# The second pair of experts is loaded without waiting for the first tile's gathered rows

## Chip, cores and metric

The kernel runs on one core of one Trainium2 chip. The metric is the device time of one execution in microseconds (us), as a median over several executions. Engines are called PE (TensorE), PEld (its weight loads), ACT (ScalarE), DVE (VectorE), POOL (GpSimd) and SP (SyncE, which here only issues DMAs). DMAs issued by SP appear as queue q1, those issued by POOL as q0.

## The reference, cut to what matters

Two transformer blocks run one after the other on 512 tokens of width 1024, in float32. The first is a state-space mixer beside forgetting attention and a gated MLP. The second is retention beside sliding-window attention, then a mixture of experts, then a gated per-layer embedding. The change concerns the mixture of experts:

```python
def hierarchical_moe(h, w_rg, b_rg, w_re, b_re, w_gate, w_up, w_down):
    ...
    g_sel = jnp.argmax(g_prob, axis=-1)                  # one of 4 groups
    ...
    top_p, top_i = lax.top_k(jax.nn.softmax(e_in_group, axis=-1), TOP_K)   # 2 of its 8 experts
    ...
    for grp in range(N_GROUPS):
        sl = slice(grp * EXPERTS_PER_GROUP, (grp + 1) * EXPERTS_PER_GROUP)
        hid = jax.nn.silu(jnp.einsum('td,edf->tef', hf, w_gate[sl])) * jnp.einsum('td,edf->tef', hf, w_up[sl])
        y = y + jnp.einsum('tef,efd->td', hid * combine[:, sl, None].astype(hid.dtype), w_down[sl])
    return y.reshape(b, s, d)
```

There are 32 experts, each with a gate and an up matrix of 1024 x 256 and a down matrix of 256 x 1024, and every token uses two of them.

## The kernel before, in words

**Up to the experts.** All dense weights stream through a ring of 8 buffers (`raw`), in units of 256 KB that SP loads. ACT and DVE split each unit into a high part (`hi`) and a low part (`lo`), and PE multiplies with both, so that a product takes three matmuls (lines 341 to 343). PE counts finished units in the semaphore `unit_used`. The stream's last units before the experts are the router's and those of the per-layer embedding (`ple0`, `ple1`). With the last matmul on `ple1` the count reaches `MOE_AT`, and from then on nobody reads `raw`, `hi` or `lo` for the whole expert stage.

**Routing.** DVE turns the router's logits into a table `sidx` of token rows for each tile of work (lines 1081 to 1183), with two small stretches of PE in between (the ranks of the tokens at line 920, the table itself at line 930). Before that POOL has stored the normalised rows `xn3` in device memory as `xg_d`.

**Expert tiles.** An expert gets up to 64 rows; two experts make a tile of 128 rows. There are `MAIN` = 16 main tiles (expert j with expert j + 16) and `OVER` = 8 overflow tiles for experts that got more than 64 rows, run in the order main, main, overflow. For tile n:
- POOL gathers its rows from `xg_d` into `XE[n % 2]` with an indirect DMA (`gather`, line 1269; semaphores `xe_full[0]` and `xe_full[1]`). Gathers 0 and 1 are issued as soon as `sidx` stands; gather n + 2 follows when PE has transposed tile n. Rows out of bounds are skipped.
- PE transposes them (`turn`, lines 934 to 941), DVE scales them into `XT` (line 1188), PE multiplies with the gate and up weights (`gate_up`, line 958: 32 matmuls), ACT and DVE form the hidden values, PE multiplies with the down weights (`down`, line 977: 16 matmuls), and POOL scatters the result to `ye_d` (line 1277).

PE's loop for tile n is gate_up(n), turn(n + 1), down(n - 1), then two transposes (line 991).

**Expert weights.** The pair j of experts has 6 MB of weights. SP loads them into one of two slots: four pieces of 1024 KB for gate and up (line 1348), then 2048 KB for down (line 1354). Slot 0 has memory of its own. Slot 1 lies over the ring, 48 KB a partition at exactly the place of `raw`, `hi` and `lo`. So pair 0 may be loaded while the dense stream still runs, and pair 1 only once `unit_used` stands at `MOE_AT`. In the kernel before, SP waits for one more thing ahead of pair 1: for `xe_full[0]`, the landing of gather 0. A later pair's piece is loaded when PE has used the same piece of the pair two before it. For overflow tiles, POOL loads weights into a third slot with indirect DMAs (line 1284) that skip everything where no expert overflows.

**Who waits for what ahead of the first gate_up.** PE waits for `xe_full[0]` in `turn(0)`, then for the count 48 of `b2c` (ACT's copies of the embedding at line 1026 raise it to 48; its later work at lines 1035 and 1039 raises it to 58), then for `XT` of tile 0, then for piece 0 of the weights:

```python
            turn(0)
            pe.wait_ge(b2c, 48)
```

The program of SP and what calls it, with the numbers of the profile's lines:

Of the kernel before, what the change touches and what calls it, by code (L numbers as in the profile page):

```python
# [69 lines left out]
def nth_split(u):  # L70

    return u if u < MOE_AT + XU else u - XU
# [30 lines left out]
def bass_two_blocks(nc, x, cst_d, rows_d, mats_d, bias_d, ident_d, identb_d, maskT_d, maskL_d, rb_d, tri_d,  # L103
                    pT_d, wstream, wexp, out):
    ctx = ExitStack()
    with ctx:
        def sem(name):
            return ctx.enter_context(nc.semaphore(name))
# [195 lines left out]
        xe_full = [sem(f"xe_full{i}") for i in range(2)]  # L304
# [1007 lines left out]
        @block.sync  # L1312
        def _(sp):
            for t in range(T):
                sp.dma_start(X[:, t, :], x[t * P:(t + 1) * P, :]).then_inc(x_loaded[t], 16)
            for c in range(RING):
                sp.dma_start(raw[:, c, :], wstream[c]).then_inc(raw_full[c], 16)

            def reload(u0, n=RING):

                for u in range(u0, u0 + n):
                    if u - RING >= MOE_AT:
                        sp.wait_ge(unit_used, u + 1 - RING)
                    else:
                        sp.wait_ge(lo_ready, u + 1 - RING)
                    sp.dma_start(raw[:, u % RING, :], wstream[u if u < MOE_AT else u - XU]).then_inc(raw_full[u % RING], 16)

            rounds = MOE_AT // RING
            with sp.Fori(1, rounds) as i:
                for c in range(RING):  # L1330
                    sp.wait_ge(lo_ready, i * RING + (c + 1 - RING))
                    sp.dma_start(raw[:, c, :], wstream[bass.ds(i * RING + c, 1)].rearrange("a p n -> (a p) n")
                                 ).then_inc(raw_full[c], 16)
            reload(rounds * RING, MOE_AT - rounds * RING)
            both = wexp.rearrange("(e m) p n -> m p e n", e=2)

            def gate_up(j):

                if j == 0:
                    sp.wait_ge(m_s, 8)  # L1340
                    sp.wait_ge(lo_ready, MOE_AT - PIECES)
                elif j == 1:
                    sp.wait_ge(unit_used, MOE_AT)
                    sp.wait_ge(xe_full[0], 16)
                for i in range(PIECES):
                    if j >= 2:
                        sp.wait_ge(unit_used, MOE_AT + (j - 2) * PIECES + i + 1)
                    sp.dma_start(slots[j % 2][:, :, 2 * i:2 * i + 2, :].rearrange("p e c n -> p e (c n)"),
                                 both[j][:, :, 1024 * i:1024 * i + 1024]).then_inc(raw_full[(j * PIECES + i) % RING], 16)

            def down(j):
                if j >= 2:
                    sp.wait_ge(dn_mm, 2 * ORDER.index(j - 2) + 2)
                sp.dma_start(slots[j % 2][:, :, 8:12, :].rearrange("p e c n -> p e (c n)"),
                             both[j][:, :, 4096:6144]).then_inc(dn_full[j % 2], 16)

            for j in range(0, MAIN, 2):
                gate_up(j)
                if j == 0:
                    down(j)  # L1360
                gate_up(j + 1)
                if j:
                    down(j)
                down(j + 1)
            sp.wait_ge(unit_used, MOE_AT + XU)
            reload(FIRST["pg0"], RING)
            for i in range(2):
                sp.wait_ge(ye_st[i], 16 * (TILES // 2))
            for t in range(T):
                sp.dma_start(YG[:, :, :].rearrange("p (k t) d -> p k t d", k=2)[:, :, t, :],  # L1370
                             ye_d.rearrange("(k t p) d -> p k t d", k=2, t=T)[:, :, t, :]).then_inc(x_loaded[t], 16)
            for u in range(FIRST["pg1"], NU):
                sp.wait_ge(lo_ready, nth_split(u - RING) + 1)
                sp.dma_start(raw[:, u % RING, :], wstream[u - XU]).then_inc(raw_full[u % RING], 16)
            for t in range(T):
                sp.wait_ge(out_ready, 4 + t + 1)
                sp.dma_start(out[t * P:(t + 1) * P, :], X[:, t, :]).then_inc(out_stored, 16)
            sp.wait_ge(out_stored, 16 * T)
# [1122 lines left out]
```

## Time and profile before

| what | value |
|---|---|
| median of 3 runs | 1678.85 us (1678.52 to 1680.55) |
| the profiled execution's own time | 1680.54 us |
| its span, from the first to the last instruction | 1678.6 us |
| mean granted clock of PE | 0.97 |
| PE busy | 1560.0 us, 93% of the span |
| DVE, ACT, POOL busy | 809.5, 617.5, 137.9 us |

The profiled execution lies 1.7 us above the median of the three runs and 1.9 us above its own span. A busy share is an average over stages with different limits, so the stage of the change is read by itself. The granted clock is the share of full speed that the chip allowed PE in a stretch; 0.50 is 1.2 GHz and 1.00 is 2.4 GHz. "To landing" is the time from the issue of a DMA to the increment of its semaphore.

### The profile page before, as it was taken

Reading aid. Unit: us, or ns where it says so; the run is one execution under the profiler, and the core shown is the slowest. Engines: PE = TensorE matmul, PEld = TensorE weight load, DVE = VectorE, ACT = ScalarE, POOL = GpSimd, SP = SyncE. Lnnn points to the kernel's source line nnn. Section 1 sums busy time; section 2 is a strip of 40 time slices with the busy share of each in tenths; the row PEclk is TensorE's granted clock in tenths of the full one; section 3 lists DMA queues with packets and bytes.
Section 4 is the critical chain, followed back from the end, with each engine's and each line's share of the span. In section 5 each row is a group of like instructions: output and inputs, shape, how many; then the busy total and the mean of one; then the engine's idle time right before and its main releaser. Section 6 shows DMA issues by size and latency. Waiting matters only on the chain.

```text
span 1678.6 us, 20983 instructions
## 1 busy us (share of the span) xinstructions
PE 1560.0 (93%) x7452; PEld 1133.3 (68%) x7452; DVE 809.5 (48%) x1472; ACT 617.5 (37%) x1182; POOL 137.9 (8%) x156
## 2 busy tenths in 40 slices
PE   5989999989999999999999998999997999999947
PEld 4777778745787888888887887777785333333336
DVE  4766764577334666664324354654456122222263
ACT  4556543367324455553223313454335200000122
POOL 0004200010000000000000001000001122221100
PEclk9999999999999999999999999999998999999969
DMA  5232233221232333333323322221243999999331
GB/s 183 69 128 90 73 120 95 60 73 39 72 98 76 96 99 94 100 94 97 99 82 102 100 70 63 70 69 59 86 170 137 407 411 400 388 386 369 129 150 50
DMA packets 93168, 232.93 MB, mean 139 GB/s; under 512 B 15952, under 2 KB 16208, under 8 KB 88864
## 3 DMA queue, kind: packets, MB, share of 16 engines
q1 hardware_dynamic: 79296, 209.75, 36.3%
q0 software_dynamic: 13072, 21.77, 3.9%
q8 instruction: 53, 0.87, 0.2%
q10 hardware_dynamic: 720, 0.33, 0.1%
q14 instruction: 27, 0.22, 0.0%
HBM read 282.05 MB, written 16.84 MB: 178 GB/s over the span
## 4 chain that ended last, share of the span: by engine, by line
PE 84%; DVE 9%; ACT 3%; issue 1%; DMA 1%; POOL 1%; SPq 0%; ACTq 0%; DVEq 0%; POOLq 0%
PE ps L341 20%; PE ps L343 19%; PE ps L342 19%; PE ps L958 10%; PE ps L977 5%; PE ps L940 1%; DVE lo L336 1%; PE ps L444 1%; DVE acc L1929 1%; PE ps L1594 1%; PE ps L1582 1%; PE ps L1568 1%; PE ps L544 1%; PE ps L1446 1%; DVE HTl L409 1%
## 5 line engine op out<-in xcount | busy, mean ns | idle before, releaser
L336 DVE TENSOR_TENSOR lo<-raw,hi 128x512 fp32r<-128x512 f32 x304 | 208.6, 710 | 313.8 <-ACT hi L330 313.2
L330 ACT ACTIVATE hi<-raw 128x512 fp32r<-128x512 f32 x304 | 184.8, 632 | 383.8 <-PE ps L343 382.4
L341 PE MATMUL ps<-HTh,lo 128*128 128x512 f32 x688 | 274.3, 399 | 20.0 <-DVE HTl L409 6.4
L342 PE MATMUL ps<-HTl,hi 128*128 128x512 f32 x688 | 271.6, 395 | 0.0
L343 PE MATMUL ps<-HTh,hi 128*128 128x512 f32 x688 | 271.5, 395 | 0.0
L341 PEld LDWEIGHTS ps<-HTh,lo 128*128 128x128 f32 x688 | 131.4, 191 | 50.9 <-DVE HTl L409 12.4
L343 PEld LDWEIGHTS ps<-HTh,hi 128*128 128x128 f32 x688 | 131.6, 191 | 28.1
L342 PEld LDWEIGHTS ps<-HTl,hi 128*128 128x128 f32 x688 | 131.6, 191 | 27.1
L341 PE MATMUL ps<-hi,HTl 128*128 128x512 f32 (+1 forms) x352 | 139.0, 395 | 2.3 <-ACT sq L617 2.0
L343 PE MATMUL ps<-hi,HTh 128*128 128x512 f32 (+1 forms) x352 | 135.2, 384 | 0.0
L342 PE MATMUL ps<-lo,HTh 128*128 128x512 f32 (+1 forms) x352 | 135.1, 384 | 0.0
L958 PE MATMUL ps<-slot,XT 128*64 128x512 f32 x512 | 116.0, 607 | 2.3 <-ACT slotO L1039 1.4
L1204 DVE TENSOR_TENSOR hid<-esg,ps 128x256 f32<-128x256 f32 x24 | 10.1, 422 | 166.6 <-ACT esg L1057 166.6
L2232 DVE TENSOR_TENSOR lo<-raw,hi 128x512 fp32r<-128x512 f32 x80 | 55.4, 693 | 71.2 <-ACT hi L1864 71.2
L1864 ACT ACTIVATE hi<-raw 128x512 fp32r<-128x512 f32 x80 | 50.6, 633 | 105.2 <-PE ps L343 104.5
L958 PEld LDWEIGHTS ps<-slot,XT 128*64 128x64 f32 x512 | 36.3, 139 | 70.9 <-issue 68.0
L1057 ACT ACTIVATE esg<-ps 128x256 f32<-128x256 f32 x24 | 9.2, 384 | 199.7 <-PE ps L958 199.7
L341 PEld LDWEIGHTS ps<-hi,HTl 128*128 128x128 f32 x352 | 67.7, 192 | 16.4 <-ACT sq L617 2.2
L342 PEld LDWEIGHTS ps<-lo,HTh 128*128 128x128 f32 x352 | 67.6, 192 | 13.7 <-issue 1.4
L343 PEld LDWEIGHTS ps<-hi,HTh 128*128 128x128 f32 x352 | 67.3, 191 | 12.8
L341 PE MATMUL ps<-hi,gl 128*128 128x512 f32 x176 | 68.5, 389 | 0.0
L342 PE MATMUL ps<-lo,gh 128*128 128x512 f32 x176 | 68.5, 389 | 0.0
(378 smaller groups left out, 2514.5 us busy)
## 6 DMA issues: line engine op xcount, KB each, us to landing
raw<-in_wstream SPq DMA_DIRECT2D x384, 256.0 KB, 2.7
slot<-in_wexp SPq DMA_DIRECT2D x64, 1024.0 KB, 14.0
slot<-in_wexp SPq DMA_DIRECT2D x16, 2048.0 KB, 15.0
cum<-cum_d POOLq DMA_DIRECT2D x16, 256.0 KB, 3.4
fcb<-fc_d POOLq DMA_DIRECT2D x16, 256.0 KB, 3.7
YG<-ye_d SPq DMA_DIRECT2D x4, 1024.0 KB, 8.8
X<-in_x SPq DMA_DIRECT2D x4, 512.0 KB, 5.6
xg_d<-xn POOLq DMA_DIRECT2D x4, 512.0 KB, 4.3
```

Of the source, the lines that this page charges most:

```text
L330: act.activation(hi[:, i % RING, :], raw[:, i % RING, :], ACT.Copy).then_inc(hi_ready, 1)
L336: dve.tensor_tensor(lo[:, i % RING, :], raw[:, i % RING, :], hi[:, i % RING, :].bitcast(F32), ALU.subtract).then_inc(lo_ready, 1)
L341: pe.matmul(o, al, bh, start=start, stop=False)
L342: pe.matmul(o, ah, bl, start=False, stop=False)
L343: return pe.matmul(o, ah, bh, start=False, stop=stop)
L409: dve.scalar_tensor_tensor(HTl[:, c, :], ps[:, c, :], col(wname, c), HTh[:, c, :].bitcast(F32), ALU.mult, ALU.subtract).then_inc(ht_lo, 1)
L444: tr = pe.transpose(ps[:, c, t * P:(t + 1) * P], xnb[:, t, c * P:(c + 1) * P], ident[:, :])
L544: mm = pe.matmul(ps[:, bank, o:o + n], sqT[r, h // 2, i * P:(i + 1) * P], skT[r, h // 4, (i + 1) * P - n:(i + 1) * P], start=True, stop=True)
L958: mm = pe.matmul(ps[CAP * e:CAP * e + CAP, 2 + n % 2, :], XT[n % 2][:, c, CAP * e:CAP * e + CAP], W[:, e, c, :], start=c == 0, stop=c == D ...
L977: mm = pe.matmul(ps[CAP * e:CAP * e + CAP, 6 + hf, :], hT[:, c * P + CAP * e:c * P + CAP * e + CAP], W[:, e, 8 + 2 * hf + c, :], start=c = ...
L1864: act.activation(hi[:, sl, :], raw[:, sl, :], ACT.Copy).then_inc(hi_ready, 1)
L2232: dve.tensor_tensor(lo[:, sl, :], raw[:, sl, :], hi[:, sl, :].bitcast(F32), ALU.subtract).then_inc(lo_ready, 1)
```

## The change

SP's wait for gather 0 ahead of the second pair's loads is removed. The wait for `unit_used` stays.

```diff
@@ -1341,7 +1341,6 @@
                     sp.wait_ge(lo_ready, MOE_AT - PIECES)
                 elif j == 1:
                     sp.wait_ge(unit_used, MOE_AT)
-                    sp.wait_ge(xe_full[0], 16)
                 for i in range(PIECES):
                     if j >= 2:
                         sp.wait_ge(unit_used, MOE_AT + (j - 2) * PIECES + i + 1)
```

No engine's instructions change in kind, number or order.

## Rows read from the trace of the kernel before

**Rows 1.** The chain of waits, 1294 to 1337 us: start us, us, what

```profile
1294.11 5.00 ACT slotO L1035 x16
1299.11 1.81 ACT slotO L1039
1301.06 9.72 PE ps L958 x32
...
1325.19 7.02 PE ps L958 x32
1332.20 1.02 PE ps L940 x8
1333.23 3.58 PE ps L977 x16
1336.81 0.37 PE ps L991 x2
```

**Rows 2.** What SP waited for from 1235 us on: us in total, times, longest

```profile
SPq L1348 <- PE ps L958: 113.8, 56, 6.5
SPq L1354 <- PE ps L977: 108.7, 14, 11.8
...
SPq L1344 <- DMA XE<-xg_d,sidx: 47.7, 1, 47.7
```

**Rows 3.** Tile slot: what the matmuls on the weights sat idle for (us, times)

```profile
  issue: 98.5, 351
  ACT slotO L1039: 3.1, 2
  DVE XT L1188: 2.2, 2
```

**Rows 4.** Timeline around gather 0: start us, us, engine, line, operation [idle before <-releaser]

```profile
1289.53 2.07 ACT L1026 ACTIVATE ple<-ps 128x512 f32<-128x512 f32 x4 [7.45 <-PE ps L343]
...
1293.36 1.09 POOL L1269 DMA_INDIRECT XE<-xg_d,sidx  x1 [26.35 <-DVE sidx L1176]
...
1297.73 1.97 PE L940 MATMUL ps<-ident,XE 128*128 128x128 f32 x8 [5.58 <-DMA XE<-xg_d,sidx]
1297.75 2.14 SPq L1348 DMA_DIRECT2D slot<-in_wexp  x4
...
1299.74 1.23 DVE L1188 TENSOR_TENSOR XT<-ps,cst 128x1024 f32<-128x1024 f32 x1 [5.75 <-PE ps L940]
```

**Rows 5.** DMAs issued 1293.3 to 1293.6 us (gather 0): x count, us to landing

```profile
XE<-xg_d,sidx POOLq DMA_INDIRECT x1, 4.3
```

**Rows 6.** The DMA issued by POOL at 1300.47 us (gather 2): x count, us to landing

```profile
XE<-xg_d,sidx POOLq DMA_INDIRECT x1, 6.8
```

**Rows 7.** Queue q0 from 1301 to 1307 us: packets, MB, share of 16 engines

```profile
q0 software_dynamic: 144, 0.00, 1.3%
```

**Rows 8.** DMAs issued 1326 to 1560 us: x count, median us to landing

```profile
ye_d<-Ye,sidx POOLq DMA_INDIRECT x20, 7.6
XE<-xg_d,sidx POOLq DMA_INDIRECT x20, 8.9
```

**Rows 9.** DMAs issued 1570 to 1580 us, expert loads over: x count, us to landing

```profile
slotO<-in_wexp,oidx POOLq DMA_INDIRECT x1, 2.1
ye_d<-Ye,sidx POOLq DMA_INDIRECT x1, 2.8
```

**Rows 10.** The gathers (line 1269), all 24: us to landing min/median/max

```profile
DMA to landing us min/median/max: 4.0/8.5/10.4
```

**Rows 11.** By stretch: us, PE, PEld, DVE, ACT, POOL busy (x), PEclk, DMA share, GB/s

```profile
1250.00:1262.00 12.00, 11.79 (x53) 9.42 (x51) 5.77 (x12) 4.09 (x7) 1.69 (x3) 1.00 1.02 394
...
1282.50:1285.80 3.30, 3.30 (x9) 2.57 (x8) 2.99 (x11) 0.00 (x0) 0.00 (x0) 0.50 0.00 0
...
1293.00:1297.70 4.70, 0.00 (x0) 0.00 (x0) 0.92 (x2) 3.59 (x11) 2.12 (x2) 0.50 0.43 113
...
1301.00:1306.40 5.40, 5.34 (x14) 1.87 (x16) 0.00 (x0) 5.38 (x2) 0.46 (x1) 0.50 1.00 373
```

## The prediction, made before the changed kernel ran

> **What bounds the kernel now.** I read the chain of waits first, for the stretch around the experts' start, and then what each engine waited for there. In the chain every tile of the expert stage has the same four pieces, all PE's: 7.02 for gate_up, 1.02 for the transposes, 3.58 for down, 0.37 for the two last transposes, 11.99 us in all [rows 1]. Nothing stands between them. What the matmuls on the slots sat idle for is issue, ACT and DVE; a DMA of weights is not in the list, in 24 tiles not once [rows 3]. The other way round, SP waited 113.8 us for PE's gate_up and 108.7 us for its down before it could load the next piece [rows 2]. So from the first gate_up on the stage is PE's, and the weights are early. An earlier load can be worth something only if somebody waits for it, and nobody does.
>
> The wait that the change removes is in SP's list as one of 47.7 us, put down to gather 0 [rows 2]. The profile names the last of two semaphores. The other one, `unit_used` at `MOE_AT`, is also what ACT's copy of the embedding waits for, and that starts at 1289.53 [rows 4]. So only some 8.2 of the 47.7 us (1289.5 to 1297.75) belong to the line removed.
>
> The critical piece is what precedes the first gate_up. The chain puts ACT's work on `slotO` there (5.00 and 1.81 us) [rows 1], and the row on the matmuls names ACT too [rows 3]. By the code this is an accident of equal times. PE needs only the count 48 of `b2c`, reached by the copies that end at 1291.6 [rows 4], and the XT of tile 0. The XT starts at 1299.74 and takes 1.23, so it ends at 1300.97, and the first gate_up starts at 1301.06 [rows 1, 4]. XT waits for the transposes, and these start at 1297.73 after PE sat idle for 5.58 us on the DMA of gather 0 [rows 4]. Gather 0 is thus on the path that sets the end: each us by which it lands later moves all 24 tiles and the tail.
>
> **Part 1: the wait goes.** SP issues pair 1's five loads from about 1289.6 instead of 1297.75. Gain on the path: 0, since PE doesn't wait for slot 1; it reads it first after gate_up 0, eight transposes and an XT, at 1301.06 + 9.72 + 1.02 + 1.23 = 1313.0 [rows 1, 4]. The later loads follow PE's counts and aren't moved ahead. Less backlog for them is worth 0 for the same reason. Bounds: 0 and 0.
>
> **Part 2: gather 0 loses its empty queue.** From 1293.36, where gather 0 is issued, to its landing 4.3 us later nothing else runs [rows 4, 5]. In the changed kernel pair 1 has been under way for some 3.7 us by then. Its 6.3 MB last 16 us at the 394 GB/s that pair 0's load shows [rows 11], from about 1290 to 1306, so they lie over the whole flight of gather 0. What a DMA of POOL takes beside such loads, three comparisons show:
> - The 20 gathers issued between 1326 and 1560 take 8.9 us in the median against 4.3 alone: +4.6 [rows 5, 8]. Most of them follow a scatter in their queue, which may add something.
> - Scatters come first in their queue: 7.6 in the median with loads, 2.8 once the loads are over, so +4.8 [rows 8, 9].
> - Gather 2 is the nearest: issued 2.7 us after the first load of pair 1, for an overflow tile without rows. Its queue moves 144 packets and 0.00 MB, and yet it lands after 6.8 us [rows 6, 7]. An indirect DMA without data takes 2.1 us alone [rows 9]: +4.7.
>
> I take +4.5, a little under the three because gather 0 has nothing ahead of it in its queue: landing at about 1293.4 + 8.8 = 1302.2 instead of 1297.7. Bounds: +2.5, if with nothing ahead it does as well as the 6.8 of gather 2; and +6.1, the slowest gather of all, 10.4 [rows 10]. Gather 1, issued 1.4 us later, would land by 1305 and is needed at about 1315: hidden.
>
> **Part 3: PE's clock.** PE's granted clock is 0.50 from 1293, while PE is idle, to 1306.4, some 5.4 us into the first gate_up [rows 11]. That is the lower of the two levels, 1.2 GHz. It makes the first gate_up 9.72 instead of 7.02 us, a cost of 2.70 [rows 1]. The changed kernel idles longer and then does the same work, so I expect the same cost, moved: 0. The shortest stretch at 0.50 nearby lasts 3.3 us [rows 11]. With one as short the first gate_up would lose 1.65 us, 1.05 less than now; with a stretch longer by half as much again (2.7 us) it would lose 1.35 more. Bounds -1.0 and +1.4.
>
> **What else could move.** ACT's squares and zeroing of `slotO` need no DMA and stay where they are, under PE's longer wait. They end near 1306, and gate_up 0 now ends at about 1315, so ACT's first silu waits for PE as before. POOL's gather 2 goes out 4.5 us later and is needed a tile later: hidden. Cost 0.
>
> **The sum.** 0 + 4.5 + 0 = +4.5 us. Against the profiled execution's own 1680.54 that is 1685.0. The median of the runs is 1.7 us below that execution, so 1678.85 + 4.5 = **1683.3 us** in a median, +0.27%. The difference that a measurement of this kernel can tell from none is about 0.2%, 3.4 us, so the forecast lies only just beyond it.
>
> **The rivals.**
>
> *A. The gather waits for one piece only (within 0.2%).* If each DMA engine takes turns between SP's and POOL's queues, gather 0 waits at most until the piece of weights in front of it is through. A piece of 1024 KB takes 1.05 MB / 394 GB/s = 2.7 us [rows 11], half that in the mean, so gather 0 is late by 1.3 to 2.7 and the time is 1680.2 to 1681.5. For it: the gather moves at most 0.5 MB. Against it: gather 2 has no data to move and is still 4.7 us slower under load than such a DMA alone [rows 6, 7, 9]. The Trainium skill ("DMA: Bandwidth & Descriptors", section "Queues, rings and completion order") states the rule behind this: an engine goes round the queues that have work and drains one packet, typically 9 to 17 descriptors, before it switches. By that rule the sum would be the one of this rival rather than mine; the trace of before agrees only if a DMA of POOL has to wait for more than one such turn. Chance 0.15.
>
> *B. The clock gives part back (within 0.2%).* The gather is late by 3 to 4.5 us, but the first gate_up catches more of the full clock, up to 1.0 us. 1678.85 + 4.5 - 1.0 = 1682.3, or 1681 with a gather at the low end. For it: of 9.72 us more than half ran at 0.50, so there is something to win. Chance 0.12.
>
> *C. Gather 0 is not disturbed (not slower).* The mechanism: what delays POOL's DMAs later on is a backlog of pieces several deep and the scatter ahead, and pair 1's five loads, alone in flight, leave gather 0's few packets a way through at its own 4.3 us. Then turn(0) starts at 1297.7 as before, the loads gain nothing, and the time is 1678.9. It decides if gather 0 lands in under about 5 us beside the loads. For it: gather 1 landed in 4.0 us [rows 10] though the loads began 3 us after its issue. Against it: that was its last us only, and gather 2 met exactly those five loads and took 6.8 [rows 6]. Chance 0.08. With a luckier clock the same case ends up to 1 us below; faster by over 0.2% would need 3.4 us that no row offers: 0.02.
>
> *D. The change does nothing.* If something else held SP until 1297, the time would be 1678.9. SP has nothing between pair 0's loads and this wait, and ACT's row shows the count reached at 1289.5 [rows 4]. Chance 0.01.
>
> **How the numbers follow.** The forecast itself, gather late by 3.4 us or more and the clock as now or worse, gets 0.62. That gives slower by over 0.2%: 0.62; within 0.2%: A, B, C and D, 0.36; faster: 0.02. The low end goes down to A's lower half, 1680.0, below which C and D lie. The high end is the slowest gather with a little of the clock's bound: 1678.85 + 6.1 + 1.0 = 1686.0.
>
> **What would show it.** In the changed kernel's profile the first load of line 1347 after the ring should start near 1289.6. Gather 0 should take 8 to 9.5 us to landing instead of 4.3. PE's wait for it should grow from 5.6 to about 10 us, and the first gate_up should start near 1305.5 instead of 1301.06, counted from a router that ends at the same time. Its length should stay between 8.7 and 11 us. From then on every tile should take 11.99 us as before, and SP should still wait for PE. I am wrong if gather 0 lands in under 6 us, if the first gate_up is much shorter than 9.7, or if any tile after the first gets shorter, which would mean that weights were late somewhere after all.

## The result, and the profile after

| | before | changed |
|---|---|---|
| median of 20 runs each | 1679.45 us | 1681.81 us |
| lowest and highest | 1675.97, 1681.09 | 1679.34, 1685.73 |
| span of the profiled execution | 1678.6 us | 1680.3 us |
| its own time | 1680.54 us | 1682.18 us |

The ratio is 1.0016, with a 95% interval of 1.0009 to 1.0022: the change costs 2.7 us (1.5 to 3.7). That is less than the 4.5 us forecast. The median lies inside the range given (1680.0 to 1686.0), and just on the near side of the 0.2% that I had called distinguishable. With e1_again below, which is the same kernel, there are 29 runs of it. Against the 84 of the kernel before that were timed in the first three sets their mean is 3.2 us higher (2.6 to 3.8), or 0.19%; with the 35 of the last set too it is 3.1 us (2.5 to 3.7).

The chain of waits of the changed kernel, around the first gate_up and one tile later (start us, us, what):

```profile
1291.34 7.68 DMA XE<-xg_d,sidx
1299.02 0.04 issue
1299.07 1.97 PE ps L940 x8
1301.04 1.36 issue
1302.40 9.90 PE ps L958 x32
...
1326.71 7.02 PE ps L958 x32
1333.73 1.02 PE ps L940 x8
1334.75 3.58 PE ps L977 x16
1338.34 0.37 PE ps L991 x2
```

The landing of gather 0 now stands in the chain by itself, as the longest piece but the gate_up. Before, the chain showed ACT's work on `slotO` in this place [rows 1], which had merely ended at the same moment as XT. That work is unchanged now and out of the chain, which is what the prediction read from the code. One tile later nothing differs: 7.02, 1.02, 3.58 and 0.37 as in [rows 1].

The timeline (start us, us, engine, line, operation; line numbers of SP are one less than before):

```profile
1285.10 2.26 SPq L1347 DMA_DIRECT2D slot<-in_wexp  x4
1285.11 2.06 ACT L1026 ACTIVATE ple<-ps 128x512 f32<-128x512 f32 x4 [5.84 <-PE ps L343]
...
1287.40 0.66 SPq L1353 DMA_DIRECT2D slot<-in_wexp  x1
1288.19 1.95 PE L930 MATMUL ps<-rowof,hot 128*64 128x48 f32 x32 [3.12 <-DVE rowof L1173]
...
1291.34 1.09 POOL L1269 DMA_INDIRECT XE<-xg_d,sidx  x1 [27.11 <-DVE sidx L1176]
...
1299.07 1.97 PE L940 MATMUL ps<-ident,XE 128*128 128x128 f32 x8 [8.94 <-DMA XE<-xg_d,sidx]
1301.08 1.23 DVE L1188 TENSOR_TENSOR XT<-ps,cst 128x1024 f32<-128x1024 f32 x1 [9.10 <-PE ps L940]
```

SP issues pair 1 within 0.01 us of ACT's copy, as the prediction took it to. PE's wait for the gather is 8.94 us instead of 5.58 [rows 4]. In this execution ACT's copy starts 4.4 us and gather 0 2.0 us earlier than in the one of [rows 4], and so gather 0 goes out 6.2 us after pair 1's first load, not some 3.8; all of that comes from work ahead of the change. So executions are compared from the issue of gather 0. From there to the end of the first gate_up is 17.4 us before (1293.36 to 1310.78) [rows 1, 4] and 21.0 now (1291.34 to 1312.30).

Gather 0 from issue to landing, where [rows 5] had 4.3, and all 20 from 1326 to 1560, where [rows 8] had 8.9:

```profile
XE<-xg_d,sidx POOLq DMA_INDIRECT x1, 7.7
...
XE<-xg_d,sidx POOLq DMA_INDIRECT x20, 8.4
```

By stretch, as in [rows 11] (us, PE, PEld, DVE, ACT, POOL busy, PEclk, DMA share, GB/s):

```profile
1291.30:1295.00 3.70, 0.00 (x0) 0.00 (x0) 0.64 (x2) 2.91 (x9) 2.12 (x2) 0.50 1.02 391
1295.00:1299.00 4.00, 0.00 (x0) 0.00 (x0) 0.00 (x0) 4.00 (x10) 0.00 (x0) 0.50 1.04 420
...
1302.40:1307.60 5.20, 5.20 (x14) 1.70 (x16) 0.00 (x0) 2.99 (x2) 2.37 (x3) 0.50 0.39 131
```

The DMA engines carry 391 to 420 GB/s during the whole flight of gather 0, where [rows 11] had 113. Afterwards they fall to 131: the load that was brought forward leaves a hole behind it, and nobody was waiting for what filled it. PE's clock is again at the lower level, 0.50, for the first half of the gate_up.

What SP waited for (us in total, times, longest), and what the matmuls on the slots sat idle for:

```profile
SPq L1347 <- PE ps L958: 128.8, 56, 18.0
SPq L1353 <- PE ps L977: 110.9, 14, 11.7
...
SPq L1347 <- PE ps L343: 37.7, 1, 37.7
```

```profile
  issue: 101.8, 353
  DVE XT L1188: 2.2, 2
```

The removed wait's row is gone; what is left of it is the wait of 37.7 us for the ring. SP's waits for PE's gate_up grew from 113.8 to 128.8 us [rows 2], the longest from 6.5 to 18.0. SP hurries to the next wait. And still no DMA of weights among the matmuls' idle time [rows 3].

### The profile page after: what moved, and what is told of

The parts are those of the page before. It is cut to its first block, busy times and chain, and to the rows that moved or that the text cites. A ratio compares the mean times of both kernels' runs of the same rounds, so it can differ in the third digit from the quotient of the medians.

```text
span 1680.3 us, 20982 instructions
## 1 busy us (share of the span) xinstructions
PE 1558.8 (93%) x7452; PEld 1133.0 (67%) x7452; DVE 809.5 (48%) x1472; ACT 617.2 (37%) x1182; POOL 137.6 (8%) x156
## 4 chain that ended last, share of the span: by engine, by line
PE 83%; DVE 10%; ACT 3%; issue 2%; DMA 1%; POOL 1%; SPq 0%; ACTq 0%; DVEq 0%; POOLq 0%
PE ps L341 20%; PE ps L343 19%; PE ps L342 19%; PE ps L958 10%; PE ps L977 5%; PE ps L940 2%; DVE lo L336 1%; PE ps L444 1%; DVE acc L1928 1%; ACT Pb L1817 1%; PE ps L544 1%; PE ps L1593 1%; PE ps L1445 1%; DVE HTl L409 1%; PE ps L1581 1%
```

## The experiments

Each was timed beside the kernel before on the same chip. "Landing" is the time from gather 0's issue to its landing in the profiled execution; "stretch" runs from that issue to the end of the first gate_up.

| run | what differs from the changed kernel | ratio to before (95%) | landing | first gate_up | stretch |
|---|---|---|---|---|---|
| (before) | | 1 | 4.3 | 9.72 | 17.4 |
| (changed) | | 1.0016 (1.0009 to 1.0022) | 7.7 | 9.90 | 21.0 |
| e1_again | nothing | 1.0025 (1.0015 to 1.0035) | 8.3 | 9.48 | 21.1 |
| e2_one_piece | one piece ahead of the wait | 0.9998 (0.9989 to 1.0007) | 4.1 | 10.04 | 17.5 |
| e3_paced | one load in flight | 0.9999 (0.9990 to 1.0008) | 4.4 | 9.72 | 17.5 |
| e4_late | pair 1 still later than before | 0.9997 (0.9988 to 1.0006) | 4.2 | 9.82 | 17.4 |
| e5_two_flight | two loads in flight | 0.9999 (0.9991 to 1.0008) | 7.5 | 9.97 | 20.8 |
| e9_two_flight_again | the same | 1.0005 (0.9996 to 1.0014) | 5.3 | 9.23 | 17.9 |
| e6_small | loads of 256 KB | 1.0023 (1.0014 to 1.0033) | 8.1 | 9.75 | 21.2 |

### Once more, and only one piece early

**e1_again** is the changed kernel.

> The changed kernel once more, unaltered, as the measure beside the three below and for a second look at gather 0. Theory G (gather 0 is slowed by the loads as any DMA of POOL is, the time follows it): gather 0 lands after 7.2 to 9 us as in the first trace (7.7), the first gate_up takes 9 to 10.5, the time is 2 to 4 us over the kernel before. Rival A (the gather waits for one piece in front of it only): 5.6 to 7.0 us to landing in this second trace, +1.3 to +2.7. Rival C (not disturbed; the first trace was chance): about 4.3 us and a time within 0.5 us of before.

+4.2 us (2.5 to 5.9), and in the chain of waits gather 0 is this:

```profile
1292.89 8.26 DMA XE<-xg_d,sidx
```

The landing is in the middle of what theory G expected, and the time just above its 2 to 4 us. Rivals A and C expected a landing of at most 7.0.

**e2_one_piece** puts the wait back behind the first piece:

```diff
                 for i in range(PIECES):
+                    if j == 1 and i == 1:
+                        sp.wait_ge(xe_full[0], 16)
                     if j >= 2:
```

> Only the first piece (1024 KB) of pair 1 goes ahead of the wait for gather 0; the other four loads wait as before. That piece is issued near 1289.6 on the clock of the first trace and lands some 6 us after its issue, its traffic over about when gather 0's data start to flow. Theory G: gather 0 lands after 4.3 to 5.0 us, time within 0.7 us of the kernel before. Rival E (something other than the loads' traffic, such as SP's earlier issue or state of the queues, slows the gather): 7 us or more and +2 to +4 us as in the changed kernel.

```profile
1289.96 4.08 DMA XE<-xg_d,sidx
```

No difference from before, at a landing of 4.1. SP's queue is as early here as in the changed kernel, with one load instead of five, so it isn't the early issue that hurts but the loads that fill gather 0's flight.

### Later still

**e4_late**, set against the kernel before:

```diff
                 elif j == 1:
                     sp.wait_ge(unit_used, MOE_AT)
-                    sp.wait_ge(xe_full[0], 16)
+                    sp.wait_ge(unit_used, MOE_AT + 1)
```

> The other direction: the wait for gather 0 is replaced by one for PE's first counted pair of matmul blocks of gate_up 0, so that pair 1 is issued about 7 us later than in the kernel before, near 1304.8. If Part 1 of the prediction holds (nobody waits for slot 1), the time stays within 1 us of before: the first piece lands at about 1311, the second gate_up starts at 1313, and only its last piece can be late, by 0 to 1.5 us. If weights are short in this stage, which would have been the reason to load them earlier, the time grows by 4 to 7 us. Gather 0 lands in 4.3 us either way, and gather 1 (4.0 to 4.3) and gather 2 (now before the loads, 2.1 instead of 6.8) too.

SP issues pair 1 at 1303.71, 11.4 us after gather 0's issue, against 4.4 in the kernel before. The time is the same (-0.5 us, between -2.0 and +1.0). Only here does a DMA of weights appear in the list of what the matmuls on the slots sat idle for:

```profile
  issue: 97.7, 348
  ACT slotO L1039: 3.1, 2
  DMA slot<-in_wexp: 2.7, 3
  DVE XT L1188: 2.2, 2
```

2.7 us over matmuls and weight loads together, 0.8 of it PE's matmuls. So the kernel before loaded pair 1 some 7 us earlier than it had to, and the changed kernel adds to a slack that was there already. Gather 2, for a tile without rows, goes out before the loads here and lands after 2.1 us, where it took 6.8 beside them [rows 6]: the same DMA, with and without loads, differs by 4.7, as the prediction had put together from two different ones.

### Backlog or traffic

**e3_paced** starts as early as the changed kernel, one load at a time (each load of gate and up raises one of the semaphores `raw_full` when it lands):

```diff
                 for i in range(PIECES):
+                    if j == 1 and i:
+                        sp.wait_ge(raw_full[PIECES + i - 1], 16 * ((MOE_AT + PIECES) // RING + 1))
                     if j >= 2:
...
+                if j == 1:
+                    sp.wait_ge(raw_full[PIECES + 3], 16 * ((MOE_AT + PIECES) // RING + 1))
                 if j >= 2:
                     sp.wait_ge(dn_mm, 2 * ORDER.index(j - 2) + 2)
```

> Pair 1 starts as early as in the changed kernel, but each of its five loads is issued only when the one before has landed, so that at most one is in flight and no backlog forms. Theory G in the form 'a backlog of pieces is what a DMA of POOL waits behind': gather 0 lands after 4.5 to 6 us, time +0 to +1.5 over before. Theory G in the form 'any load traffic at the time does it': 6.5 us or more, +2 or more. Rival A (one piece in front at most) expects no difference from the changed kernel, since one piece is all that it waits for: the same landing as in e1_again and the same time. In all of them pair 1 lands by about 1320, its down part at 1322; the second gate_up may wait up to 1 us.

No loss, and a landing of 4.4. But the stretches say why this is less than it seems (columns as above):

```profile
1291.00:1293.20 2.20, 1.03 (x32) 0.90 (x32) 1.09 (x3) 0.47 (x1) 0.00 (x0) 0.89 0.95 346
1293.20:1294.50 1.30, 0.00 (x0) 0.00 (x0) 0.64 (x2) 0.51 (x1) 1.09 (x1) 0.50 0.37 151
1294.50:1296.00 1.50, 0.00 (x0) 0.00 (x0) 0.00 (x0) 1.50 (x7) 1.03 (x1) 0.50 0.58 137
1296.00:1297.70 1.70, 0.02 (x1) 0.03 (x1) 0.00 (x0) 1.70 (x7) 0.00 (x0) 0.50 1.03 357
```

Between two pieces the engines are about half free (137 to 151 GB/s, a DMA share of 0.37 and 0.58, from 1293.2 to 1296.0), and gather 0, issued at 1293.24, had this gap for most of its flight. It doesn't tell backlog from traffic. Gather 1, issued 1.4 us later, met one piece and took 6.2 us.

**e5_two_flight** and **e9_two_flight_again** close the gap:

```diff
                 for i in range(PIECES):
+                    if j == 1 and i >= 2:
+                        sp.wait_ge(raw_full[PIECES + i - 2], 16 * ((MOE_AT + PIECES) // RING + 1))
                     if j >= 2:
...
+                if j == 1:
+                    sp.wait_ge(raw_full[PIECES + 2], 16 * ((MOE_AT + PIECES) // RING + 1))
                 if j >= 2:
                     sp.wait_ge(dn_mm, 2 * ORDER.index(j - 2) + 2)
```

> In the paced kernel one piece at a time left gaps of some 2 us between pieces, and gather 0 fell into one, so it didn't tell backlog from traffic. Here pair 1's loads start as early as in the changed kernel and at most two are in flight: each is issued when the one two before it has landed. The traffic should have no gap (over 330 GB/s from 1291 to 1301), and only the depth of the backlog differs from the changed kernel (five). Theory 'traffic' (what counts is that the engines are busy when the gather comes): 7 to 8.5 us to landing, +2 to +4 us, as in the changed kernel. Theory 'backlog' (a DMA of POOL waits behind what was already queued): 5.3 to 6.8 us, +1 to +2.5. Gather 1, which met one piece in the paced kernel, took 6.2 there against 9.1 to 9.6 in the changed kernel, which speaks for the backlog.

> The kernel with two loads in flight once more, unaltered. Its first trace showed gather 0 landing 7.5 us after its issue and a start of gate_up as late as in the changed kernel, but that execution (1681.7) was the slowest of the 12 timed ones, whose median was that of the kernel before. Theory 'backlog': most executions land gather 0 in 4.5 to 6 us, this second trace with some luck too, and the time is +0 to +1.5 again. Theory 'traffic': 7 to 8.5 us again, and then the median ought to be +2 to +4, and the first time was chance.

The stretches of the second one while gather 0 (1292.54 to 1297.8) was in flight:

```profile
1293.00:1295.00 2.00, 0.00 (x0) 0.00 (x0) 0.18 (x1) 1.71 (x5) 1.66 (x2) 0.50 0.97 363
1295.00:1297.00 2.00, 0.00 (x0) 0.00 (x0) 0.00 (x0) 2.00 (x9) 0.00 (x0) 0.50 1.04 395
```

```profile
XE<-xg_d,sidx POOLq DMA_INDIRECT x1, 5.3
```

The engines are about as full as in the changed kernel (a DMA share of 0.97 and 1.04, there 1.02 and 1.04), and gather 0 lands after 5.3 us instead of 7.7 to 8.3. The first trace, of the slowest of the twelve executions, had 7.5. In time the two runs together are 23 executions with a median of 1679.2 us, against 1679.4 for the kernel before beside them (1679.46 and 1679.25); the means differ by 0.4 us (-0.3 to +1.2). Full engines alone don't explain the loss, then; with no more than two loads in flight it is mostly gone. It isn't gone in each execution, as the trace with 7.5 shows, and what decides between 5.3 and 7.5 stays open. In that execution gather 0 was issued 6.2 us after the first load, in the other 3.9; in both two loads were under way at that moment. Gather 1, behind gather 0 in its queue, took 8.1 and 7.5 us.

**e6_small** cuts pair 1's gate and up pieces into four DMAs each:

```diff
+                    if j == 1:
+                        for h in range(4):
+                            e, c = h // 2, 2 * i + h % 2
+                            sp.dma_start(slots[1][:, e, c, :], both[1][:, e, 512 * c:512 * c + 512]
+                                         ).then_inc(raw_full[(PIECES + i) % RING] if h == 3 else small_full, 16)
+                        continue
```

> The changed kernel with each of the four gate and up pieces of pair 1 cut into 4 DMAs of 256 KB, with rows of 2 KB instead of 4 KB in each partition; same bytes, same start. If engines serve the queues in turns and a turn is as long as a load's share or a packet of its descriptors (Rival A and its rule), the turns are now half to a quarter as long and gather 0 lands after 4.7 to 6 us, +0.5 to +1.7 us. If the wait is set by busy engines and memory, 7 to 8.5 us as in the changed kernel and +2 to +4. SP issues 16 loads in about 8 us, so the backlog is shallower too: a short landing here counts for turns only as far as it is below that of the kernel with two in flight.

+3.9 us (2.4 to 5.5), a landing of 8.1. That speaks against turns whose length is the size of a DMA or of its rows: both were cut, and nothing was won. (PE's wait for pair 1 was fitted to the new semaphore; its loads had landed long before it.) It is also a warning for the backlog reading. SP issued these sixteen loads over 8.67 us. When gather 0 went out 3.85 us after the first, nine had been issued and two had landed; seven were on their way, 1.8 MB, and some ten, 2.6 MB, when the last of the sixteen was issued. In e9 it was at most two, up to 2.1 MB, in e1_again five, 6.3 MB. If bytes on their way counted, e6 should have been nearer to e9 than to e1_again. The number of loads would fit all three; no run varied it alone, so that is a guess.

Where in its flight gather 0 loses the time, the packets of POOL's queue q0 show. In the kernel before its first packet moves 1.7 us after the issue. In the changed kernel and in e1_again it moves after 4.4 us (from 1291.4 to 1295.6, 437 packets of q1 and none of q0), in e6_small after 4.8, with two loads in flight after 2.8 (e9) and 3.5 (e5). So 2.7 of the 3.4 us that the changed kernel's profiled execution lost had passed before a packet of the gather moved; the rest was lost while they moved. What holds the first packet back is not shown.

### PE's clock out of the way

Extra matmuls (identity times identity into a bank that nobody reads) keep PE busy in its three waits (the numbers are those of e10):

```diff
+            def warm(k):
+
+                for _ in range(k):
+                    pe.matmul(ps[:, 3, 0:P], ident[:, :], ident[:, :], start=True, stop=True)
+
+            warm(4)
             pe.wait_ge(map_ready, 1)
...
+            warm(20)
             turn(0)
+            warm(4)
             pe.wait_ge(b2c, 48)
```

| run | made from | extra matmuls | median (interval of its ratio to before) | landing | first gate_up | stretch |
|---|---|---|---|---|---|---|
| e7_warm_before | before | 12, 36, 8 | 1680.97 (0.9990 to 1.0014) | | 7.09 | 16.7 |
| e8_warm_after | changed | 12, 60, 8 | 1682.45 (1.0012 to 1.0032) | | 7.09 | 22.1 |
| e10_warm2_before | before | 4, 20, 4 | 1676.03 (0.9966 to 0.9984) | 4.2 | 7.09 | 13.8 |
| e11_warm2_after | changed | 4, 34, 4 | 1679.24 (0.9994 to 1.0011) | 9.1 | 7.42 | 19.8 |
| e12_alone | e10, gather 1 after gather 0 | 4, 20, 4 | 1675.48 (0.9971 to 0.9988) | 4.3 | 7.09 | 13.9 |

> The kernel before, with PE kept busy while it waits: 12, 36 and 8 extra matmuls (identity times identity, 128 columns, into bank 3 that nobody reads) ahead of the table's matmuls, ahead of turn(0) and ahead of the first gate_up. It tests Part 3: the clock is low because PE stood idle, and that costs 2.7 us of the first gate_up and 0.9 of turn(0). Expected: granted clock 1.00 from 1286 to the first gate_up, which takes 7.0 to 7.3 us; time 2.5 to 4 us under the kernel before. If the clock falls for another reason the extra matmuls run at half speed, last 9 us instead of 4.6 and cost up to 5 us.

> The same for the changed kernel, with 60 instead of 36 extra matmuls for its longer wait. With the clock out of the way its distance from e7_warm_before is gather 0's lateness alone: theory 'lateness passes on in full' expects +3.4 to +3.9 us between the two (7.7 and 8.2 us to landing against 4.3), more than the 2.7 (1.5 to 3.7) that the changed kernel lost in the timed runs if the clock gave some back there; Rival B (the clock gives part back) expects just that: more than in the kernels without extra matmuls. If the distance is the same as without them, the clock gave nothing back.

A miss of mine: there were too many. In e7 PE worked on extra matmuls when gather 0 had landed long since:

```profile
1292.82 8.30 PE L930 MATMUL ps<-ident 128*128 128x128 f32 x72
1300.96 1.04 PE L946 MATMUL ps<-ident,XE 128*128 128x128 f32 x8
...
1303.72 7.09 PE L966 MATMUL ps<-slot,XT 128*64 128x512 f32 x32
```

8.30 us for 36 of them, 0.23 each. I had priced them by the transposes of line 940, 1.02 us for 8 [rows 1]. Yet the gate_up took 7.09 as expected. In time e7 gained nothing, where 2.5 to 4 us were expected. The pair can't measure the lateness either: turn(0) waited for the extra matmuls in both, starting 6.9 us after gather 0's issue in e7 and 12.2 in e8, so their distance of 3.6 us (1.5 to 5.6), though close to the forecast, isn't gather 0's lateness alone. The two were sized anew.

> The extra matmuls of the last two runs took 0.23 us each, not 0.13 as I had reckoned, so 36 of them lasted 8.3 us and held turn(0) up by 3.2 us; the first gate_up took 7.09 as forecast. Here their numbers fit the gaps: 4, 20 and 4 (0.9, 4.6 and 0.9 us). Expected: turn(0) starts on gather 0's landing (4.3 us), the first gate_up takes 7.1, time 2.5 to 4 us under the kernel before.

The stretches of e10, to be set beside [rows 11]:

```profile
1288.40:1292.40 4.00, 3.37 (x52) 3.12 (x51) 2.69 (x6) 2.06 (x4) 0.00 (x0) 1.00 0.00 0
1292.40:1296.60 4.20, 3.47 (x32) 3.28 (x30) 0.62 (x2) 3.43 (x11) 2.12 (x2) 1.00 0.42 116
...
1299.00:1306.10 7.10, 7.01 (x32) 2.65 (x32) 0.00 (x0) 7.08 (x3) 0.52 (x2) 1.00 1.00 368
```

PE is at 1.00 (2.4 GHz) through its whole wait, and the stretch falls from 17.4 to 13.8. The time is 0.9975 of before, 4.2 us less (2.7 to 5.7): the lower clock after the wait for gather 0 cost 2.6 us in the gate_up (9.72 against 7.09) and 0.9 in the transposes (1.97 [rows 4] against 1.09), which is nearly all of what the stretch lost.

> The changed kernel with 4, 34 and 4 extra matmuls (0.9, 7.8 and 0.9 us). Its distance from e10_warm2_before is gather 0's lateness with PE's clock out of the way. If lateness passes on in full: +3.2 to +4.5 between the two. If the clock gave part back without the extra matmuls, the distance grows beyond the 3.2 that all timed runs of the changed kernel together show; if it is 3.2 again, the clock's part was nil.

e11 is 4.5 us slower than e10 in the mean (2.9 to 6.1). Gather 0 takes 9.1 against 4.2, +4.9, which fits a lateness that passes on in full; it is one trace of each. The extra matmuls ended 2.6 us before the landing here, the clock fell once more, and the transposes took 1.55, which accounts for a part of the rest of the stretch. Against the 3.2 without extra matmuls the intervals overlap: a gift from the clock in the changed kernel isn't shown.

> e10_warm2_before plus the opposite of the change: gather 0 gets the queue even more to itself, in that POOL issues gather 1 only when gather 0 has landed. If gather 1 behind it costs gather 0 anything, it now lands in 3.3 to 4.0 instead of 4.3 us, and the time is 0.3 to 1.0 under e10. Gather 1 then meets pair 1's loads, takes 7 to 9 us from 1297.7 and lands by 1307, before turn(1) near 1309. If gather 1 is late, turn(1) waits and the time is over e10's.

```diff
             gather(0)
+            pool.wait_ge(xe_full[0], 16)
             gather(1)
```

```profile
1290.37 4.32 DMA XE<-xg_d,sidx
...
1295.47 9.41 DMA XE<-xg_d,sidx
```

A miss: gather 0 lands after 4.3 us without anything behind it too, so gather 1 had cost it nothing. Gather 1 now meets pair 1's five loads and takes 9.4, the change's effect once more, on the next gather, and PE waits 0.65 us for it. Only two of the five loads had been issued when gather 1 was, the other three within 1.7 us after it, and yet its first packet moved only after 4.7 us. So it isn't only what stood in the queue before the gather that delays it. In time e12 and e10 can't be told apart. Both beat the kernel before and the changed one.

## Why the prediction was right, and where not

**The bound** was read rightly. Nobody waited for the weights (Part 1: 0). e4_late shows it from the other side: 7 us later still costs nothing.

**The path** was read rightly, against what the chain of waits put there. Gather 0 leads to turn(0), XT and the first gate_up; the changed kernel's chain has it in the open.

**Gather 0's price (Part 2)** is the term that was mis-sized: +4.5 forecast, +3.4 in the profiled execution (7.7 against 4.3), +4.0 in e1, +3.2 us (2.6 to 3.8) in the time of all runs. The three comparisons gave 4.6 to 4.8, from gathers and scatters inside the steady stage and from gather 2. Where it failed is the step "I take +4.5, a little under the three": the nearest row, gather 2 with five loads begun just before, was 6.8 in all, +2.5, and I kept it as the lower bound only. The measured value lies between the two. The landing itself, forecast at 8 to 9.5 us, was 7.7 and 8.3. That nothing else runs beside gather 0 in the kernel before overlooked gather 1, issued 1.4 us after it; e12 shows that it costs gather 0 nothing.

**The clock (Part 3)**: 0 forecast, bounds -1.0 and +1.4. The first gate_up took 9.90 and 9.48 against 9.72: +0.2 and -0.2. Its cause, PE's idleness ahead of it, is shown by e10.

**Rival A**, that gather 0 waits for one piece only, is refuted as to its mechanism: both traces lie above its 7.0 us, and with loads a quarter as large (e6) the landing doesn't shrink. The 2.7 us that the changed kernel's gather lost before its first packet are just what A reckoned for one piece of 1024 KB, but with pieces of 256 KB they were 3.1. Its time, 1680.2 to 1681.5, lay nearer to the measured 1681.81 than mine did; a price can be right with a wrong reason. The rule on turns between queues that the Trainium skill states ("DMA: Bandwidth & Descriptors", section "Queues, rings and completion order") isn't shown wrong: several turns for one gather would also give more than one piece's time. No run here counts turns. **B** isn't shown, **C** is refuted (7.7, 8.3), **D** too (SP issues at 1285.10).

**The chances**: slower by over 0.2% had 0.62, and the 20 runs say 0.16%, inside what had 0.36. With an effect of 3.2 us and a line at 3.4 the side on which it falls is close to even. The direction and the range were right.

## What to carry to other kernels

Before you let a large load start earlier, ask two things: who waits for it, and what small DMA is in flight at that time that somebody does wait for. Here a wait that looked like 47.7 us of idling on SP protected a gather whose landing moves the whole expert stage. If such a load has to start early, keep few DMAs of it in flight, which here took the loss away in time, though not in each trace; and if the engine on the path must idle for a few us, keep it busy with work nobody reads, which was worth 4.2 us (2.7 to 5.7) here, once the number of extra matmuls fitted the waits, and nothing when there were too many.

## What the runs showed of the hardware beyond what I expected

- An indirect gather of 128 rows took 4.1 to 4.4 us on free or half-free engines and 7.7 to 9.1 with four or five loads of 1 to 2 MB on their way, of which 2.7 us were added before its first packet moved. With at most two queued it took 5.3 in one execution and 7.5 in another, though the engines moved 363 to 395 GB/s around the faster one.
- Loads a quarter of the size, with rows of 2 KB instead of 4 KB, delayed the gather as much (8.1).
- A matmul of 128x128 on 128 columns in fp32 took 0.23 us at full clock, a transpose of the same shape 0.13.
- PE's clock stayed at 1.00 through 5 us of waiting that extra matmuls filled, where it had fallen to 0.50 without them.
